# Expert weights requested in the order their buffers come free, and the down product's two column halves side by side in the array

## The reference, cut to what matters

```python
def expert_block(args):
    tok_b, e = args
    xb = xpad[tok_b]
    h = jax.nn.silu(xb @ w_gate[e]) * (xb @ w_up[e])     # (1024 x 512) each
    return h @ w_down[e]                                 # (512 x 1024)
...
out = out.reshape(rows, d) * buf_wt[:, None].astype(out.dtype)
y = jnp.zeros((t + 1, d), out.dtype).at[buf_tok].add(out)[:t]
```

## Time and profile before

| | |
|---|---|
| Median of 3 runs | 2018.04 us (2014.17 to 2018.47) |
| Profiled execution, span from first to last instruction | 2013.0 us |
| Its time outside of that span | not recorded by itself; the median is 5.0 us above the span |
| TensorE busy | 1784.1 us (89%) |
| VectorE busy | 1320.9 us (66%) |
| ScalarE busy | 706.7 us (35%) |
| GpSimd busy | 451.8 us (22%) |
| Granted TensorE clock, mean of the span | 0.940 |
| DMA, whole span | 406.90 MB, mean 202 GB/s |
| Expert stage, first product to last down product | about 177 to 792 us |

### The profile page before, as it was taken

One profiled execution on the slowest core, in us unless ns is written; L12 is line 12 of the kernel. 1 busy time (PEld: TensorE's weight loads), 2 busy tenths in 40 slices (PEclk: granted clock), 3 DMA queues, 4 the chain that ended last, 5 costly groups with the idle time before them and its releaser, 6 DMA issues. The chain is left out here.

```text
span 2013.0 us, 25709 instructions
## 1 busy us (share of the span) xinstructions
PE 1784.1 (89%) x9316; PEld 1377.1 (68%) x9316; DVE 1320.9 (66%) x1466; ACT 706.7 (35%) x929; POOL 451.8 (22%) x257
## 2 busy tenths in 40 slices
PE   6986998998998997778898995999997669999997
PEld 6855445444454453567768995999997558888886
DVE  3336666666666662385521799666667988888886
ACT  4514555555555552333413331222216750000000
POOL 6511110110110110462214583000006960000000
PEclk9997999999999998888898997999999989999999
DMA  8326799999899996552140352555552005555554
GB/s 289 117 102 244 287 359 348 342 345 348 319 348 349 343 343 211 184 190 84 58 152 21 135 180 84 188 179 180 183 188 83 0 0 191 199 195 188 190 197 144
DMA packets 139559, 406.90 MB, mean 202 GB/s; under 512 B 10616, under 2 KB 13816, under 8 KB 123000
## 3 DMA queue, kind: packets, MB, share of 16 engines
q1 hardware_dynamic: 136408, 395.77, 55.5%
q10 hardware_dynamic: 3104, 10.49, 1.4%
HBM read 396.80 MB, written 10.35 MB: 202 GB/s over the span
## 5 line engine op out<-in xcount | busy, mean ns | idle before, releaser
L1964 DVE TENSOR_TENSOR ring_rest<-ring,w_lead 128x2048 fp32r<-128x2048 f32 x128 | 291.7, 2320 | 148.7 <-ACT w_lead L1099 148.5
L1099 ACT ACTIVATE w_lead<-ring 128x2048 fp32r<-128x2048 f32 x128 | 237.8, 1903 | 172.7 <-issue 68.2
L2182 DVE TENSOR_TENSOR rest<-raw,lead 128x2048 fp32r<-128x2048 f32 x112 | 256.8, 2293 | 3.9
L2174 DVE CAST lead<-raw 128x2048 fp32r<-128x2048 f32 x112 | 137.4, 1227 | 153.2 <-PE bank L1691 98.9
L1448 PE MATMUL bank<-ring,hT 128*64 128x512 f32 x512 | 229.3, 601 | 1.2 <-issue 1.2
L710 POOL TENSOR_TENSOR ring_rest<-ring,half_lead 128x2048 fp32r<-128x2048 f32 (+1 forms) x38 | 172.6, 4555 | 246.4 <-ACT half_lead L704 246.2
L1493 PE MATMUL bank<-w_lead,x_two 128*128 128x512 f32 x512 | 165.2, 460 | 42.5 <-ACT w_lead L1099 35.3
L1493 PEld LDWEIGHTS bank<-w_lead,x_two 128*128 128x128 f32 x512 | 99.2, 211 | 105.5 <-ACT w_lead L1099 62.6
L1448 PEld LDWEIGHTS bank<-ring,hT 128*64 128x64 f32 x512 | 68.1, 138 | 146.4 <-issue 146.4
L615 ACT ACTIVATE xhat<-h 128x1024 f32<-128x1024 f32 x6 | 6.3, 1057 | 456.7 <-DVE h L2249 360.7
L1493 PE MATMUL bank<-ring_rest,x_two 128*128 128x512 f32 x512 | 149.0, 427 | 16.8 <-DVE ring_rest L1964 16.7
(11 more groups left out here) (318 smaller groups left out, 2827.6 us busy)
## 6 DMA issues: line engine op xcount, KB each, us to landing
ring<-in_w_gate SPq DMA_DIRECT2D x32, 2048.0 KB, 13.9
ring<-in_w_up SPq DMA_DIRECT2D x32, 2048.0 KB, 18.8
ring<-in_w_down SPq DMA_DIRECT2D x32, 2048.0 KB, 8.8
raw<-in_u SPq DMA_DIRECT2D x64, 1024.0 KB, 4.8
raw<-in_v SPq DMA_DIRECT2D x64, 1024.0 KB, 4.8
ring<-in_w_in SPq DMA_DIRECT2D x14, 2048.0 KB, 11.6
ring<-in_w_out SPq DMA_DIRECT2D x4, 2048.0 KB, 7.6
y_sorted<-y_blk ACTq DMA_DIRECT2D x32, 256.0 KB, 6.9
```

The lines of the kernel that those rows point to most:

```text
L1099: act.activation(w_lead[half][:, :, :], ring8(slot)[:, 4 * half:4 * half + 4, :], ACT.Copy).then_inc(w_lead_ready, 1)
L1964: dve.tensor_tensor(ring_rest8(slot)[:, part, :], ring8(slot)[:, part, :], w_lead[half][:, :, :].bitcast(F32), ALU.subtract).then_inc(w_re ...
L2174: return dve.tensor_copy(dst, src)
L2182: dve.tensor_tensor(rest[slot][:, :], raw[slot][:, :], lead[b][:, :].bitcast(F32), ALU.subtract).then_inc(rest_ready, 1)
```

## The change

Three things are done in the path that runs.

1. SP asks for weights in the order gate(e), up(e), down(e - 1): the load of a down matrix for j = 1 moves from the end of a pair to the middle of the next one, and that for j = 0 to the end of the pair. The first six loads are put in the order 0, 1, 3, 4, 2, 5.
2. The down product writes both column halves into one bank (6 + j): half 0 into partitions 0 to 63, half 1 into partitions 64 to 127, with the matmuls of the halves alternating. It waits for the copy of two experts before. Its counter goes up once, by two, at the end.
3. The output tile is 128x512. ScalarE copies it in one instruction and issues two stores of 128 KB, one for each half; VectorE's copy is gone.

The path for more than 64 tokens is adapted to match (`y_many`, counters per expert).

```diff
-            for i in range(RING):
+            for i in (0, 1, 3, 4, 2, 5):
                 src, k = expert_source(i, 0)
                 load(CH_MOE + i, src, k=k)
-            with sp.Fori(1, PAIRS) as pair:
-                for i, (j, kind) in enumerate(PAIR):
-                    s = (CH_MOE + i) % RING
-
-                    if kind == 2:
-                        sp.wait_ge(down_done, 4 * pair + 2 * j - 2)
-                    else:
-                        sp.wait_ge(w_used, 4 * pair + 2 * j + kind - 3)
-                    src, k = expert_source(i, pair)
-                    dst = ring[s][:, :].rearrange("p (k f) -> p k f", k=k)
-                    sp.dma_start(dst, src).then_inc(ring_full[s], 16)
+            def reload(i, pair):
+                j, kind = PAIR[i]
+                if kind == 2:
+                    sp.wait_ge(down_done, 4 * pair + 2 * j - 2)
+                else:
+                    sp.wait_ge(w_used, 4 * pair + 2 * j + kind - 3)
+                src, k = expert_source(i, pair)
+                dst = ring[W_SLOT[i]][:, :].rearrange("p (k f) -> p k f", k=k)
+                sp.dma_start(dst, src).then_inc(ring_full[W_SLOT[i]], 16)
+
+            for i in (0, 1, 3, 4, 2):
+                reload(i, 1)
+            with sp.Fori(2, PAIRS) as pair:
+                reload(0, pair)
+                reload(1, pair)
+                reload(5, pair - 1)
+                reload(3, pair)
+                reload(4, pair)
+                reload(2, pair)
+            reload(5, PAIRS - 1)
...
                 def copy_store(e, pair, j, peeled):
-                    act.wait_ge(down_done, 2 * e + 1)
+                    act.wait_ge(down_done, 2 * e + 2)
                     if not peeled:
-                        act.wait_ge(y_stored, 16 * e - 16)
-                    act.activation(y_blk[j][:, 0:512], bank[6][0:BLOCK, :], ACT.Copy).then_inc(y_act, 1)
+                        act.wait_ge(y_stored, 32 * e - 32)
+                    act.activation(y_blk[j][:, :], bank[6 + j][:, :], ACT.Copy).then_inc(y_act, 1)
                     first = act.value_load(starts_i[0:1, bass.ds(e, 1)], min_val=0, max_val=SLOTS)
                     act.wait_ge(y_act, e + 1)
-                    act.wait_ge(y_dve, e + 1)
 
                     if j or not peeled:
-                        act.wait_ge(y_stored, 16 * e)
-                    act.dma_start(y_sorted[bass.ds(first, BLOCK)], y_blk[j][:, :]).then_inc(y_stored, 16)
+                        act.wait_ge(y_stored, 32 * e)
+                    for half in range(2):
+                        act.dma_start(y_sorted[bass.ds(first, BLOCK), half * 512:(half + 1) * 512],
+                                      y_blk[j][half * BLOCK:(half + 1) * BLOCK, :]).then_inc(y_stored, 16)
...
+            def expert_out_both(dst, w, hidden_t):
+
+                for f in range(4):
+                    for half in range(2):
+                        last = pe.matmul(dst[half * BLOCK:(half + 1) * BLOCK, :], hidden_t[:, f, :],
+                                         ring4(w)[:, f, half * 512:(half + 1) * 512], start=(f == 0), stop=(f == 3))
+                return last
...
                     pe.wait_ge(hT_ready, e + 1)
-                    for half in range(2):
-                        if not first:
-                            pe.wait_ge((y_act, y_dve)[half], e)
-                        expert_out(half, W_SLOT[3 * j + 2], hT[j]).then_inc(down_done, 1)
+                    if not first:
+                        pe.wait_ge(y_act, e - 1)
+                    expert_out_both(bank[6 + j], W_SLOT[3 * j + 2], hT[j]).then_inc(down_done, 2)
...
-                def expert_vector(e, j, peeled, former_peeled):
+                def expert_vector(e, j):
                     split_rest(e, j, 0)
-                    if not peeled:
-                        copy(e - 2, j, former_peeled)
                     split_rest(e, j, 1)
```

More of the change, by code:

```diff
@@ L284, in build @@
         hT = [acts(f"hT{j}", [P, 4, BLOCK], 48 + j) for j in range(2)]
-        y_blk = [acts(f"y_blk{j}", [BLOCK, D], 8 + 4 * j) for j in range(2)]
+        y_blk = [acts(f"y_blk{j}", [P, 512], 8 + 2 * j) for j in range(2)]
+        y_many = acts("y_many", [BLOCK, D], 12)
         slot_wt = acts("slot_wt", [P, SLOTS // P, T], 72)
@@ L1077, in many_scalar @@
                             act.wait_ge(many_stored, 16 * n)
-                        act.activation(y_blk[0][:, 0:512], bank[6][0:BLOCK, :], ACT.Copy).then_inc(y_act, 1)
+                        act.activation(y_many[:, 0:512], bank[6][0:BLOCK, :], ACT.Copy).then_inc(y_act, 1)
                         act.wait_ge(y_act, n + 1)
                         act.wait_ge(y_dve, n + 1)
-                        act.dma_start(y_sorted[bass.ds(first + b * BLOCK, BLOCK)], y_blk[0][:, :]).then_inc(many_stored, 16)
+                        act.dma_start(y_sorted[bass.ds(first + b * BLOCK, BLOCK)], y_many[:, :]).then_inc(many_stored, 16)
                 many_scalar(0, True)
@@ L1086, in _ @@
                 act.wait_ge(many_stored, 16 * N_EXPERTS * BLOCKS_MAX)
-                act.nop().then_inc(y_stored, 16 * N_EXPERTS)
+                act.nop().then_inc(y_stored, 32 * N_EXPERTS)
             with act.Else():
@@ L1156, in _ @@
                 copy_store(N_EXPERTS - 1, PAIRS - 1, 1, False)
-            act.wait_ge(y_stored, 16 * N_EXPERTS)
+            act.wait_ge(y_stored, 32 * N_EXPERTS)
             for b in range(2):
@@ L1455, in many_products @@
                 def many_products(pair, peeled):
-                    for i in range(RING):
-                        pe.wait_ge(ring_full[W_SLOT[i]], pair_fill(pair, i))
                     for j in range(2):
                         w_g, w_u, w_d = W_SLOT[3 * j:3 * j + 3]
+                        for kind in range(3):
+                            pe.wait_ge(ring_full[W_SLOT[3 * j + kind]], pair_fill(pair, 3 * j + kind))
                         for b in range(BLOCKS_MAX):
@@ L1472, in many_products @@
                                 expert_out(half, w_d, hT[0]).then_inc(many_down, 1)
-                    pe.wait_ge(many_down, 2 * (2 * pair + 2) * BLOCKS_MAX)
-                    pe.nop().then_inc(w_used, 4)
-                    pe.nop().then_inc(down_done, 4)
+                        pe.wait_ge(many_down, 2 * (2 * pair + j + 1) * BLOCKS_MAX)
+                        pe.nop().then_inc(w_used, 2)
+                        pe.nop().then_inc(down_done, 2)
                 many_products(0, True)
@@ L1522, in _ @@
                 product(2, 0, 1, False)
-                down(1, 0, 1, False)
+                down(1, 0, 1, True)
                 product(3, 1, 0, False)
@@ L1951, in many_vector @@
                             dve.wait_ge(many_stored, 16 * n)
-                        dve.tensor_copy(y_blk[0][:, 512:], bank[7][0:BLOCK, :]).then_inc(y_dve, 1)
+                        dve.tensor_copy(y_many[:, 512:], bank[7][0:BLOCK, :]).then_inc(y_dve, 1)
                 many_vector(0, True)
@@ L1971, in total @@
                                              ALU.add).then_inc((gate_sum, up_sum)[kind], 1)
-                def copy(e, j, peeled):
-                    dve.wait_ge(down_done, 2 * e + 2)
-                    if not peeled:
-                        dve.wait_ge(y_stored, 16 * e - 16)
-                    dve.tensor_copy(y_blk[j][:, 512:], bank[7][0:BLOCK, :]).then_inc(y_dve, 1)
-                def expert_vector(e, j, peeled, former_peeled):
+                def expert_vector(e, j):
                     split_rest(e, j, 0)
-                    if not peeled:
-                        copy(e - 2, j, former_peeled)
                     split_rest(e, j, 1)
@@ L1988, in expert_vector @@
                     dve.tensor_tensor(hid[j][:, :], hid[j][:, :], upv[j][:, :], ALU.mult).then_inc(hid_ready, 1)
[L1990 to L1994, removed]
+                with dve.Fori(0, PAIRS) as pair:
                     for j in range(2):
-                        expert_vector(2 * pair + j, j, False, False)
-                for j in range(2):
-                    copy(N_EXPERTS - 2 + j, j, False)
+                        expert_vector(2 * pair + j, j)
             for use in range(4):
```

## The result

The changed kernel takes 1917.0 us (median of 4 runs, 1915.9 to 1921.0) against 2016.1 us (2011.7 to 2018.5) for the kernel before: a ratio of 0.952, interval 0.950 to 0.955. In a later session it was 1919.3 against 2010.8, 0.953 (0.950 to 0.956). The forecast was 1946 with a range from 1926 to 1982, so the time is 29 us under the forecast and 9 us under the range. The profiled execution took 1920.95 us with a span of 1919.2, 93.8 us less than before.

The account below looks back on a forecast made before the run. TensorE's chain and weight requests were taken to hold each other back. Rate 45 us, start 11 and end 16 made the stage 72.2 us shorter: span 1940.8 plus 5.0, 1946 us; range 1926 to 1982.

Parts of the forecast that it names:

- What bounds the kernel now.: In the expert stage, SP's weight requests wait for down products and the queues drain; 15 pauses sum to 48.0 us.
- The down product and the overlap.: On TensorE, the two column halves overlap nearly wholly: 3.6 us instead of 7.1, bounds 3.5 and 7.1.
- The chain of one expert.: From down product through copy and stores to up: a step without waits for weights goes from 17.0 to 14.4 us.
- The rate of the stream.: Weights and stores move at 376 GB/s, bounds 360 and 390; 17.4 us per expert, the only bound.
- The start.: Of the 13 us pause before the gate of expert 3 flows, some 1.8 us stay; this gives 11 us.
- The end.: After the last weights: last down product ends at 716.2, `y_rows` asked for at 723.6; 16 us of the gain.
- The sum.: The stage ends 72.2 us earlier: span 1940.8 us, plus 5.0 us for the median above the span, 1946 us.
- A: Rival: the down product's halves do not overlap for 512 columns, the chain stays at 17.0 us; about 1957 us, chance 0.06.
- B: Rival: requests are in time, but a chain still stands in the stream, steps of 18.0 us; 1984 us, chance 0.12.
- C: Rival: without pauses the weight stream sustains only 360 GB/s or less; 1969 us or a little more, chance 0.07.
- D: Rival: requests do not hold the queues, asking earlier only lengthens the queue; no change, 2018 us, chance 0.02.
- E: Rival: TensorE, less busy in the stage, gets a lower clock; at 0.60 steps of 21.0 us, 2088 us, chance 0.04.

Follow-up runs that it names:

- the lighter stream: The changed kernel with only half of each down matrix loaded from pair 1 on; 1877.5 us, 0.932 of the kernel before.
- the one with the halves alone: The changed kernel with the old order of requests on SP, keeping halves side by side, one copy and two stores; 1933.5 us, 0.960 of the kernel before.

## Why the prediction was wrong in size

**What bounds the kernel now.** Right. The pauses were there, and the spans differ by what the stage lost.

**The down product and the overlap.** Right: 3.6 us predicted, 3.65 measured, and the pairs of another stage were enough to read it from.

**The chain of one expert.** Right: 14.4 us predicted, 14.55 measured where nothing else binds. Up was to begin 3.2 us after the down product's end; with the lighter stream it begins 3.28 us after it (413.79 to 417.07).

**The rate of the stream.** This is the step that failed. I took 376 GB/s "near the fastest long stretch, as the slow ones contain the ends of bursts", with 390 as the upper bound. The stream ran at 395 to 396, outside of both. 196.8 MB take 497 us at 396 GB/s instead of 523.4: 26 us. The fast stretches were not free of dips either. Their DMA share of 1.01 looks full, but that column counts the time of packets, not bytes. One burst of the kernel before, asked for at 452.21, shows it:

```profile
456.00:464.00 8.00, 5.65 (x24) 3.78 (x23) 5.19 (x4) 4.58 (x4) 0.00 (x0) 0.93 1.01 371
...
460.00:461.00 1.00, 0.45 (x2) 0.41 (x3) 0.47 (x1) 1.00 (x2) 0.00 (x0) 1.00 0.98 186
...
465.00:470.00 5.00, 5.00 (x14) 2.27 (x14) 2.96 (x5) 3.63 (x5) 1.81 (x2) 0.88 1.04 390
```

Where nothing disturbs it, the burst moves 390 GB/s. But as its down matrix lands, at 461.0, it falls to 186 GB/s for a microsecond, at a share of 0.98, although SP had put in gate and up of the same burst by 457.7. The hand-over from the burst before, at 455 to 456, ran at 399. The fastest stretch of the earlier trace rows holds such a dip too, near 577. In the changed kernel, and in the one with the halves alone, no half microsecond from 300 to 400 us is under 300 GB/s. So these dips, not only the ends of bursts, stood in the 377 GB/s, and they go when the queue no longer drains; why they occur is not shown by any run. The same error put the upper end of the rate at 390 and so the lower end of the time at 1926.

**The start.** Right: 1.8 us of the pause were to stay, 1.75 did.

**The end.** Predicted 7.4 us from the last down product to the request for `y_rows`, measured 3.8 (697.75 to 701.55): the store of expert 30 had landed at 698.4, as the copy of the last output ended, and held next to nothing up.

**The sum.** The request for `y_rows` came 22 us earlier than predicted (701.55 against 723.6). The rate gives 25.8 of these up to the last up matrix, and the end 3.6. Against this, the first request came 1.75 us later than before (185.84 against 184.09), ScalarE began on the last up matrix at 680.3, 4.6 us after what the bytes and that request give, and from there to the last down product's end it took 1.0 us more than predicted; why it landed later was not tried. The other 7 us of the miss of 29 have nothing to do with the kernel: I added 5.0 us to the span, the distance of a median from one profiled execution before. The profiled execution of the changed kernel took 1.75 us more than its span and was the slowest of four, so that the median lies 2.2 us under that span. That the 26 us of the rate come near the whole miss is chance. A smaller slip: the turn and copy behind 710.8 end at 712.4 by the prediction's own terms, not 712.6.

**The steps.** 18.75 us is an average over 31 steps of which the last, with no gate or up product in it, is 9.34 us; the other 30 average 19.06. They are not alike: short ones, down to 17.02 us, alternate with long ones of up to 22.07. The prediction read one short step and took it for the chain.

**The rivals.** A (no overlap, 1957) did not happen, and its price was wrong: it kept a chain of 17.0 us, but the kernel with everything but the overlap has steps of 16.23 us and takes 1926.6. B (a chain stands in the stream), C (360 GB/s without pauses) and D did not happen. C is refuted by 396 GB/s over 467 us. The Trainium skill's page "DMA: Bandwidth & Descriptors" (section "Where 436 GB/s comes from") has transfers from HBM to SBUF bound at about 358 GB/s for a core; with one core running, as here, the trace disagrees by the same 396 GB/s. E (the clock): TensorE's busy share in the stage fell to 84%, but the granted clock was 0.97, and where more of its work was left out and the clock fell to 0.86, the time was the same.

**What the prediction had not seen.** It treated the new order as the cause and the down product's change as its support. The runs say that either alone does much of it, 61 and 80 of 99 us, and that within the second the removal of VectorE's copy counts for more than the overlap: 48 us against 32 in the kernel before, 26 against 7 to 10 under the new order. I had written that VectorE's copy "lay in front of the up remainder", and counted no more for it than the 0.7 us of the copy; its cost was on ScalarE, which waited for it behind the gate remainder. The step of the earlier trace rows does not show this, as the copy runs there 0.5 us after the down product. The next step, whose down product ends at 452.18, does:

```profile
452.63 4.49 DVE L1964 TENSOR_TENSOR ring_rest<-ring,w_lead 128x2048 fp32r<-128x2048 f32 x2 [4.42 <-ACT w_lead L1099]
...
457.04 0.68 DVE L1977 COPY y_blk<-bank 64x512 f32<-64x512 f32 x1
...
457.92 0.49 ACTq L1128 DMA_DIRECT2D y_sorted<-y_blk  x1
...
458.59 3.71 ACT L1099 ACTIVATE w_lead<-ring 128x2048 fp32r<-128x2048 f32 x2 [3.57 <-issue]
```

VectorE copies 4.9 us after the down product's end, and ScalarE begins up 6.4 us after it instead of 2.0. It is so at every second expert: 15 of the 32 copies begin 2.95 to 4.9 us late.

## What to carry to other kernels

When two loops hold each other (requests wait for compute, compute waits for data), a change on either side can free both, so gains measured or predicted for the parts do not add; price each part with the other in place. Read a queue's full rate from a short stretch in which it is surely backed up (390 GB/s here, 396 to come), and look into a longer one for dips before calling it full; the share column does not tell them, it is 0.98 at 186 GB/s. When steps alternate between short and long, read one of each. And when one engine's hand-over waits for a small instruction on another, price the queue in front of that instruction, not the instruction.

## What the runs showed of the hardware that was not expected

- A stream of 2 MB loads from memory to SBUF, with stores of 128 KB among them, ran at 396 GB/s over 467 us, on one core.
- The share of DMA time says little of the rate near full: 0.98 at 186 GB/s, 1.03 at 384 and 1.04 at 396 GB/s.
- SP's issue instruction is held while its queue is backed up, up to 10.5 us here, while ScalarE's issues of stores in the same time take 0.49 us each and land in 5.4 us: the long queue of one engine does not delay the issue of the other.
- Accumulations into opposite column halves overlap nearly fully when they alternate (3.65 us for 16 recorded matmuls, which start in pairs 0.43 us apart), and in part when four matmuls of one half come first (5.42 us).
